# Input projection of a hybrid SSD and attention block: chunks in paired form, halves added at eviction

## What is computed

```python
xn = rmsnorm(h, norm1_g[i])
proj = xn @ w_in[i]
z, xbc, dt_raw, q, k, v = jnp.split(proj, list(IN_SPLITS), axis=-1)
xbc = jax.nn.silu(causal_depthwise_conv(xbc, conv_w[i], conv_b[i]))
...
y_ssd = ssd_scan(...)                       # Mamba-2 chunked scan, 16 heads
y_ssd = y_ssd * jax.nn.silu(z)              # then a grouped rmsnorm
y_att = swa_sink_attention(q, k, v, attn_sinks[i])
h = h + jnp.concatenate([y_ssd, rmsnorm(y_att)], axis=-1) @ w_out[i]
h = h + peer_ffn(rmsnorm(h), ...)           # 16384 single-neuron experts, top 16 of 8 heads
```

## Time and profile before

| | us |
|---|---|
| median of 3 runs (1727.21 to 1727.44) | 1727.36 |
| the profiled execution, its own time | 1727.27 |
| its span in the trace | 1725.5 |
| TensorE (PE) busy | 1708.7 |
| VectorE (DVE) busy | 1334.7 |
| ScalarE (ACT) busy | 923.5 |
| GpSimd (POOL) busy | 535.3 |

### The profile page before, as it was taken

How to read it: one execution, slowest core, us unless ns; L and a number is a source line. 1 busy time by engine, 2 the same in 40 slices (tenths; PEclk the granted TensorE clock), 3 DMA queues, 4 the chain that set the end, 5 groups by cost and what they waited for, 6 DMA issues and landing times.

```text
span 1725.5 us, 27461 instructions
## 1 busy us (share of the span) xinstructions
PE 1708.7 (99%) x9931; PEld 1502.0 (87%) x9931; DVE 1334.7 (77%) x2193; ACT 923.5 (54%) x1582; POOL 535.3 (31%) x336
## 2 busy tenths in 40 slices
PE   9999999999999999999999999999999999999997
PEld 8999999988888888888888888888888888888885
DVE  7888878777999999555555666668878888888887
ACT  6545755444555555544444444455555555555556
POOL 0000000000007787778772000058545422212210
PEclk9999999999999999999999999999999999999999
DMA  7654568786657788888787888899999999999984
GB/s 259 213 202 161 169 187 281 223 245 213 201 193 194 189 195 203 198 194 192 201 193 207 259 263 267 268 360 338 366 338 359 358 365 356 362 366 357 368 331 140
DMA packets 186548, 445.77 MB, mean 258 GB/s; under 512 B 59360, under 2 KB 94448, under 8 KB 177904
## 3 DMA queue, kind: packets, MB, share of 16 engines
q1 hardware_dynamic: 146976, 373.47, 64.4%
q0 software_dynamic: 39504, 71.55, 15.6%
HBM read 423.79 MB, written 20.57 MB: 258 GB/s over the span
## 4 chain that ended last, share of the span: by engine, by line
PE 97%; DMA 1%; DVE 1%; ACT 0%; SPq 0%; issue 0%; DVEq 0%
PE ps L1748 30%; PE ps L1752 16%; PE ps L2130 7%; PE ps L2128 7%; PE ps L2126 7%; PE ps L2114 7%; PE ps L2116 7%; PE ps L1965 3%; PE ps L1966 3%; PE ps L1967 3%; PE ps L1782 3%; PE ps L1784 2%; PE ps L1783 2%; DMA big<-x_t 1%; PE ps L2079 0%; DMA raw<-w_in 0%
## 5 line engine op out<-in xcount | busy, mean ns | idle before, releaser
L964 DVE TENSOR_TENSOR low<-raw,high 128x1024 fp32r<-128x1024 f32 x378 | 461.0, 1224 | 82.6 <-ACT high L646 72.8
L1748 PE MATMUL ps<-acts,high 128*128 128x512 f32 x2048 | 488.8, 391 | 0.0
L1748 PEld LDWEIGHTS ps<-acts,high 128*128 128x128 f32 x2048 | 376.3, 188 | 72.9
L646 ACT ACTIVATE high<-raw 128x1024 fp32r<-128x1024 f32 x378 | 394.1, 1050 | 74.4 <-PE ps L1967 35.8
L639 ACT ACTIVATE high<-raw 128x1024 fp32r<-128x1024 f32 x172 | 182.6, 1062 | 171.5 <-PE ps L2130 166.6
L1752 PEld LDWEIGHTS ps<-acts,low 128*128 128x128 f32 x2048 | 262.6, 191 | 10.0
L600 POOL DMA_INDIRECT big<-v_tab,half_sb x64 | 116.7, 1824 | 489.8 <-DVE big L1653 289.8
L1752 PE MATMUL ps<-acts,low 128*128 128x256 f32 x2048 | 265.6, 283 | 0.0
L971 DVE TENSOR_TENSOR low<-raw,high 128x1024 fp32r<-128x1024 f32 x172 | 206.5, 1222 | 64.4 <-ACT high L639 63.6
L580 POOL DMA_INDIRECT gate_scratch<-gates_sb,cells_sb x128 | 204.8, 1600 | 66.2 <-issue 66.2
L869 ACT ACTIVATE side<-ps 128x256 f32<-128x256 f32 x128 | 49.1, 384 | 275.9 <-PE ps L1752 273.9
(11 more groups left out here) (293 smaller groups left out, 3036.1 us busy)
## 6 DMA issues: line engine op xcount, KB each, us to landing
raw<-u_tab SPq DMA_DIRECT2D x256, 512.0 KB
raw<-v_tab SPq DMA_DIRECT2D x172, 512.0 KB
raw_more<-v_tab SPq DMA_DIRECT2D x84, 512.0 KB
raw<-w_in SPq DMA_DIRECT2D x62, 512.0 KB
raw<-w_out SPq DMA_DIRECT2D x32, 512.0 KB
raw<-w_q SPq DMA_DIRECT2D x32, 512.0 KB
gate_scratch<-side SPq DMA_DIRECT2D x32, 384.0 KB, 5.8
big<-gate_scratch SPq DMA_DIRECT2D x16, 768.0 KB, 7.4
```

Of the source, the lines that this page charges most:

```text
L646: nc.scalar.activation(slot(high, s), slot(raw, s), ACT.Copy).then_inc(hi_done, 1)
L964: V.tensor_tensor(slot(low, s), slot(raw, s), slot(high, s).bitcast(F32), ALU.subtract).then_inc(lo_done, 1)
L1748: mm(both, tile_of(high, kk), both_of(kk), start=(kk == 0), stop=False, skip_group_check=True)
```

## The change

The 5th to the 23rd chunk of the input projection (c of 4 to 22) run in the paired form. ScalarE copies the second half of the bank to a new single buffer `in_low` (`copy_low`), and `take_in` on VectorE waits for the copy, adds the halves and multiplies, as two instructions with a wait between. In the conv part the copy of c-1 stands between the first tap and high cut 1 of c+1; in the z part, of z chunk s-1, between the two high cuts.

```diff
-Q_COPIES = 2 * PEER_HEADS - 1
+PAIRED_FROM = 4
+IN_COPIES = C_Q - PAIRED_FROM
+Q_COPIES = IN_COPIES + 2 * PEER_HEADS - 1
...
+        in_low = view(E_AT + 4 * BLK + 16, T)
...
+            def copy_low(c):
+
+                if c >= PAIRED_FROM:
+                    act.wait_ge(used, 2 * c + 2)
+                    act.wait_ge(taken, c)
+                    nc.scalar.activation(in_low, ps[:, early_bank.get(c, c % 2), T:2 * T], ACT.Copy).then_inc(lo_copied, 1)
+
...
                 cut_high_piece(c + 1, (c + 1) % 2, 0)
                 for k in convs(c):
                     first_tap(k)
+                copy_low(c - 1)
                 cut_high_piece(c + 1, (c + 1) % 2, 1)
...
             decays(0)
             for s in range(SSD_TILES):
-                cut_high(C_Z + s + 1, (C_Z + s + 1) % 2)
+                cut_high_piece(C_Z + s + 1, (C_Z + s + 1) % 2, 0)
+                copy_low(C_Z + s - 1)
+                cut_high_piece(C_Z + s + 1, (C_Z + s + 1) % 2, 1)
                 if s < SSD_TILES - 1:
                     decays(s + 1)
...
             cut_one(C_Q + 1, 0)
+            copy_low(C_Q - 1)
             cut_one(C_Q + 1, 1)
...
+            def take_in(c, dst):
+
+                bank = early_bank.get(c, c % 2)
+                if c < PAIRED_FROM:
+                    take(c, bank, dst, rstd1)
+                    return
+                dve.wait_ge(lo_copied, c - PAIRED_FROM + 1)
+                own.step(V.tensor_tensor(dst, ps[:, bank, 0:T], in_low, ALU.add))
+                own.settle()
+                V.tensor_tensor(dst, dst, rstd1, ALU.mult).then_inc(taken, 1)
...
             def take_z(s):
-                take(C_Z + s, (C_Z + s) % 2, view(QZ + (SSD_TILES + s) * T, T), rstd1)
+                take_in(C_Z + s, view(QZ + (SSD_TILES + s) * T, T))
...
-                both = ps[:, par, :]
+                both = ps[:, early_bank[c] if isinstance(c, int) and c in early_bank else par, :]
...
-            product(4, 0)
+            product(4, 0, paired=True)
```

More of the change, by code:

```diff
@@ L1055, in take_chunk @@
                     m = conv_tile(c)
-                    take(c, early_bank[c] if c in early_bank else c % 2, conv_in[:, m, CONV_W - 1:CONV_W - 1 + T], rstd1)
+                    take_in(c, conv_in[:, m, CONV_W - 1:CONV_W - 1 + T])
                 else:
-                    take(c, c % 2, k_t if c == C_K else v_t, rstd1)
+                    take_in(c, k_t if c == C_K else v_t)
             x, n, e, r, p = dtv
@@ L1442, in query_step @@
                 else:
-                    dve.wait_ge(lo_copied, m)
+                    dve.wait_ge(lo_copied, IN_COPIES + m)
                     own.step(V.tensor_tensor(q_t[j], ps[:, (C_WQ + j) % 2, 0:T], q_low[j], ALU.add))
@@ L1877, in _ @@
             product(3, 1, sum_x)
-            product(4, 0)
+            product(4, 0, paired=True)
             turn_dt()
-            product(5, 1)
+            product(5, 1, paired=True)
             with pe.Fori(3, 5) as i:
                 for j in range(2):
-                    product(2 * i + j, j)
+                    product(2 * i + j, j, paired=True)
             cumulate()
-            product(10, 0)
+            product(10, 0, paired=True)
             c_by_b()
-            product(11, 1)
-            product(12, 0)
+            product(11, 1, paired=True)
+            product(12, 0, paired=True)
             turn_cs()
             turn_x(0)
-            product(C_K, C_K % 2)
+            product(C_K, C_K % 2, paired=True)
             turn_x(1)
-            product(C_V, C_V % 2)
+            product(C_V, C_V % 2, paired=True)
             def y_of(s):
@@ L1912, in _ @@
                     y_of(s - 1)
-                product(C_Z + s, (C_Z + s) % 2)
+                product(C_Z + s, (C_Z + s) % 2, paired=True)
                 if s == 0:
```

## The result

The changed kernel takes 1735.28 us (median of 6 executions, 1733.81 to 1736.86) against 1727.28 for the kernel before (6 executions, 1726.80 to 1727.87). The ratio is 1.0047, with a 95% interval of 1.0037 to 1.0058: slower, by 8.0 us. Forecast was 1734.2, with 1731.9 to 1737 around it.

What follows compares the result with a forecast made beforehand. TensorE bounds the kernel, with a hidden ScalarE-VectorE ring as long as its lap. Lengthened, the ring delays the last y_of by 6.9 us and TensorE's 4.2 bring nothing: 1727.3 + 6.9 = 1734.2 us, range 1731.9 to 1737.

Steps and rivals of the forecast that it cites:

- The lap: z part: the take with its copy joins the ScalarE-VectorE ring of waits, so a lap goes from 6.79 to 7.87 us.
- The prices from the query stage: Take's cost, read from the query stage: 0.41 us copy to add, 0.46 add to multiply; 0.34 hand-on from another VectorE take.
- The start: First z step: its weighs end at 107.3 us instead of 105.29, 2.02 later, so TensorE waits from the first step.
- the load behind the broadcast: Before the z part: a raw load, late behind the broadcast of cs, adds 0.3 us, between 0 and 0.65.
- Where TensorE would be at the first y_of: Start of the z part: TensorE would be there at 105.8 us, counted back from the last y_of at 155.61.
- TensorE's gain: 19 paired input-projection chunks: 5.78 to 5.56 us each, 0.22 a chunk, 4.2 us in all, spent waiting for the ring.
- Conv, K and V: Input projection before z: 1.2 us more in VectorE's step fits its idle time with 0.2 to spare; costed at nothing.
- After z: First Q chunk: take at about +9.1 us from y_of, needed at +9.62; nothing more lost, or up to 2 us.
- rival B: Attention part: VectorE's 2 us lag is not made up, costing up to 2 more, 1736.2; with C 0.12.
- The clock: z part: clock should hold despite 17% idle; rival D, a fall to 1.2 GHz, would give 1775 us, chance 0.04.

Runs made afterwards that it cites:

- copy first: Changed kernel with ScalarE's copy of a z chunk ahead of high cut 0 instead of behind it; 1728.62 us, ratio 1.0007.
- segs first: Changed kernel with the copy ahead of high cut 0 and also VectorE's two segs for the next step ahead of low cut 1; 1724.65 us, ratio 0.9985.
- the run without the multiply: Changed kernel with the takes of the eight z chunks doing the add alone, leaving z unscaled; 1730.90 us, ratio 1.0020.
- the second trace: The changed kernel run once more, nothing altered, for another trace; 1735.31 us.
- the first trace: The profiled execution of the changed kernel, nothing altered; 1736.6 us.
- the four parts: Changed kernel with the 3 MB broadcast of cs cut into four, each issued when the one before has landed; 1732.91 us, ratio 1.0033.

## Why the prediction was right

**The lap.** Forecast 7.87, measured 7.84 to 7.85 in three traces. The prices from the query stage hold in the z part within a hundredth: copy to add 0.40, add to multiply 0.46, multiply to low cut 0.34. What the sum rested on was not a price, though, but the order: which instruction stands behind which on an engine that does them in turn. Swapping two (copy first) or moving one pair (segs first) took 0.8 and 0.5 a lap off; moving the copy to VectorE, into its gap, took 1.06 off.

**The start.** This term was mis-sized. I had put 0.3 us, with bounds of 0 and 0.65, on the load behind the broadcast, and the first y_of at 107.4. With the load at 91.27 it was 107.97, with 92.51 it was 109.21. Counted from its true landing the sum holds: 107.4 + (91.27 - 90.64) is 108.0, and 107.4 + 1.87 is 109.3. The step that failed is the reason behind this term, a broadcast issued later: it was issued at 78.10 and 78.44 in the two traces, against 78.44 before, and the load came 2.2 and 0.9 us later all the same. I took one trace's landing for a fixed number. It varies from one execution to the next, with and without the change: the same cut started between 88.04 and 92.51, and where it was early, the next half was the one that came late (at 94.07 in the run without the multiply). In the second trace, which is at the median, this makes 0.6 of the 1.1 us by which the forecast is too low; another 0.6 comes after z (below), and the laps take 0.2 off.

Where TensorE would be at the first y_of came out by luck. I had 105.8, counted back from the last y_of with seven laps of 6.74, but the first lap takes 7.19 (before, from 107.98 to 115.17), and I had 0.22 a chunk where it is 0.18. The two errors are 0.45 and 0.5 us and cancel: where nothing waits, it is there at 105.83 and 105.96.

**TensorE's gain.** Forecast 0.22 a chunk, 4.2 us. Measured 0.18 to 0.19: 27.83 against 28.77 us for five, and laps of 6.56 against 6.74 where nothing waits. On the basis on which an unpaired chunk takes 5.78 ((28.77 + 0.12)/5), a paired one takes 5.59 here, 0.03 more than the expert stage's 5.56. The estimate from the Trainium skill (TensorE: Matmul & The Clock Gate, "Wait — 56ns, not 53.3ns?"), 0.04, is further off. As forecast, none of it reached the end of the changed kernel.

**Conv, K and V.** Costed at nothing for TensorE, and no product waited up to K: it starts at 87.54, 1.8 us earlier than before, about 2 were forecast. VectorE's idle time ahead of low cut 1 there fell from 1.62 to 0.40 us; 0.2 was forecast. I missed that the product of V waits for the take of chunk 12, which stands behind the late load's low cut: 1.9 us in the first trace, 0.3 in the second, none with the four parts. It costs nothing on top, since the first y_of waits for VectorE anyway.

**After z.** The take of the first Q chunk came at +9.01 from y_of (forecast +9.1), and logits at +9.62 as before. What I had at nothing is 0.6: the first transposes of the attention part (line 1966) wait for VectorE. They wait for the shares of the exponentials (line 1265), which come late behind ScalarE. That is rival B at a third of its price. It sums up: 8.5 at the last y_of and 0.6 are 9.1 of the 9.3 us between the profiled executions.

**The clock.** It stayed at its upper level of 2.4 GHz: the window over the z part of the changed kernel, in the form of the earlier trace rows, has a granted clock of 1.00, with TensorE busy 47.83 of 56 us and standing 0.8 to 1.4 us ahead of each y_of.

```profile
109.00:165.00 56.00, 47.83 (x293) 39.21 (x293) 44.51 (x89) 24.98 (x39) 0.00 (x0) 1.00 0.42 142
```

The swing of which the Trainium skill (TensorE: Matmul & The Clock Gate, "A second HAM failure mode: psum-queue depth-cycling") warns did not come here. The ground on which I had it stay was thin, though: the idle time of the first 5 us lies in one piece, 1.14 us ahead of the first matmul, and says little of idle times between groups.

## What to carry to other kernels

Before adding an instruction to an engine that is "only 80% busy", write down the ring of waits through it and its partner, from one lap's row to the next, and see whether the new instruction stands on it or in one of its gaps; the ring's length against the bounding engine's lap decides, not the busy share. A ring that is as long as the bound but runs ahead of it is hidden and costs nothing until something lengthens it, and then, once its head start is used up, it shows at full price in every lap. Where a step of the ring waits for a transfer, read its landing in more than one execution before taking it as a number.

## What the runs showed of the hardware

A 3 MB broadcast on one queue, issued while 512 KB loads of another queue were due, held one of them up so that ScalarE waited up to 4.7 us, by a different amount and not always at the same load in each execution. In four parts, one after the other, it held up none that ScalarE waited for in three traces, and the spread of six executions of the changed kernel fell from 3.1 to 0.8 us.
